# The SSM gate with its weights stationary, and bias rows written in eight transfers

## The reference, cut to what matters

```
y = gelu(y.reshape(bsz, L, SSM_WIDTH))                # SSM_WIDTH = 1024
y_ssm = y * sigmoid(y @ w_glu)                        # the gate, w_glu is 1024 x 1024
logits = q k^T * HEAD_DIM ** -0.5 + rel_bias[bucket]  # 16 heads, window 128
mixed = concat([rmsnorm(y_attn, attn_out_g), rmsnorm(y_ssm, ssm_out_g)])
x = x + mixed @ w_out
```

## Time and profile before

| | |
|---|---|
| median of 3 runs | 3362.72 us (3361.55 to 3363.08) |
| the profiled execution | 3362.97 us, of which its span 3360.9 us |
| mean granted TensorE clock | 0.984 |
| weights and all else read from HBM | 588.54 MB, 177 GB/s over the span |

### The profile page before, as it was taken

The page is one execution under the profiler, slowest core; times in us unless marked ns, Lnnn a source line. Parts: engine busy times, 40 slices in busy tenths (PEclk is TensorE's granted clock), DMA queues, the critical chain, the costliest instruction groups (busy, mean ns, idle before and its releaser), DMA issues. The chain is left out here.

```text
span 3360.9 us, 38629 instructions
## 1 busy us (share of the span) xinstructions
PE 3249.7 (97%) x15842; PEld 2672.1 (80%) x15842; DVE 1866.8 (56%) x1982; ACT 1473.6 (44%) x1759; POOL 80.3 (2%) x75
## 2 busy tenths in 40 slices
PE   7897999999999999999999999999999999999998
PEld 5775788888888778878888888878787788888886
DVE  6555555555545544665555555565555655555555
ACT  5534454444444444444444444444444544444443
POOL 1020000000000000000000000000000000000000
PEclk9998899999999999999999999999999999999999
DMA  7433355555555555555555555555454555555554
GB/s 192 139 108 119 125 188 188 189 190 195 191 188 192 183 170 188 194 165 198 191 191 188 188 188 188 189 165 186 140 175 161 175 186 190 189 188 188 188 188 150
DMA packets 187548, 596.28 MB, mean 177 GB/s; under 512 B 12491, under 2 KB 19308, under 8 KB 186860
## 3 DMA queue, kind: packets, MB, share of 16 engines
q1 hardware_dynamic: 187372, 593.82, 54.3%
HBM read 588.54 MB, written 5.23 MB: 177 GB/s over the span
## 5 line engine op out<-in xcount | busy, mean ns | idle before, releaser
L1086 DVE TENSOR_TENSOR LO<-RAW,HI 128x1024 fp32r<-128x1024 f32 (+1 forms) x1104 | 1346.6, 1222 | 1146.4 <-ACT HI L580 1144.2
L580 ACT ACTIVATE HI<-RAW 128x1024 fp32r<-128x1024 f32 (+1 forms) x1104 | 1159.0, 1052 | 1371.0 <-PE PS L1905 1354.1
L1905 PE MATMUL PS<-HI,KPA 128*128 128x512 f32 x5376 | 1497.4, 395 | 15.1 <-DVE JK L1732 4.3
L1905 PEld LDWEIGHTS PS<-HI,KPA 128*128 128x128 f32 x5376 | 1008.4, 190 | 229.2 <-issue 13.0
L1905 PE MATMUL PS<-HI,KPB 128*128 128x512 f32 x3392 | 935.9, 392 | 3.5 <-DVE ACC L1619 3.4
L1905 PE MATMUL PS<-LO,KPA 128*128 128x512 f32 x2688 | 840.5, 393 | 7.6 <-DVE LO L1086 6.3
L1905 PEld LDWEIGHTS PS<-HI,KPB 128*128 128x128 f32 x3392 | 631.6, 188 | 132.8 <-issue 5.0
L1905 PEld LDWEIGHTS PS<-LO,KPA 128*128 128x128 f32 x2688 | 508.5, 190 | 120.6 <-DVE LO L1086 9.0
L1905 PE MATMUL PS<-LO,KPB 128*128 128x512 f32 x1696 | 525.0, 391 | 0.0
L1905 PEld LDWEIGHTS PS<-LO,KPB 128*128 128x128 f32 x1696 | 318.7, 188 | 68.2 <-issue 0.5
L607 ACT ACTIVATE KPB<-PS 128x512 fp32r<-128x512 f32 x98 | 58.5, 598 | 181.3 <-PE PS L1930 181.3
(11 more groups left out here) (255 smaller groups left out, 962.3 us busy)
## 6 DMA issues: line engine op xcount, KB each, us to landing
RAW<-in_w_up SPq DMA_DIRECT2D x128, 1024.0 KB, 5.1
RAW<-in_w_down SPq DMA_DIRECT2D x128, 1024.0 KB, 5.5
RAW<-in_w_qkv SPq DMA_DIRECT2D x48, 1024.0 KB, 5.1
RAW<-in_w_ff_gate SPq DMA_DIRECT2D x88, 512.0 KB, 3.7
RAW<-in_w_ff_up SPq DMA_DIRECT2D x88, 512.0 KB, 4.6
RAW<-in_w_ff_down SPq DMA_DIRECT2D x44, 1024.0 KB, 5.5
RAW<-in_w_in_ab SPq DMA_DIRECT2D x40, 1024.0 KB, 4.9
RAW<-in_w_in SPq DMA_DIRECT2D x16, 1024.0 KB, 5.2
```

Of the source, the lines that this page charges most:

```text
L580: e.activation(HI[:, s % NSPLIT, 0:w], RAW[:, d % NRAW, j, 0:w], ACT.Copy).then_inc(S("hi_made"), 1)
L1086: e.tensor_tensor(LO[:, h, 0:w], RAW[:, d % NRAW, j, 0:w], HI[:, h, 0:w].bitcast(F32), ALU.subtract).then_inc(S("lo_made"), 1)
L1905: ins = e.matmul(PS[:, b + j, 0:cw], l, r[:, h, 512 * j:512 * j + cw], start=(i == 0 and part == 0), stop=(last and part == 2))
```

## The change

It has two parts. **Bias rows:** the one DMA at L511 becomes eight, of two rows each, put behind the weight pairs of u steps 6, 8, 10, 12, 14 and q steps 0, 2, 4. RB, OH and WV get memory of their own, since WV is read for longer; ScalarE's wait at L689 goes, and SyncE's waits ask for 128 in place of 16. **Gate:** in unit glu the weights (HI, LO) are the stationary side and the y chunk of 256 tokens moves; a step is 24 products of 256 columns, each with another stationary 128x128, into banks 0 to 3, with channels on partitions. It waits for HI, LO and both halves of the chunk before its first product. The sigmoid is taken in four pieces, the first three as their bank is done, and multiplied with yT; ScalarE and VectorE make the sT pairs straight from that, without transposes. Squares are taken per pair, and 16 products with a column of ones sum them over channels.

```diff
-        add("sT", 4, ("a", 4), "q", gain="ssm_g")
+        add("sT", 4, ("a", 4), "q", turned=False, gain="ssm_g")
...
+    RB, OH, WV = (sb(n, [128, w]) for n, w in (("RB", 16), ("OH", 383), ("WV", 383)))
+    ONE = sb("ONE", [128, 1])
...
-            if d == dma_of("u", 8):
+            if dma_of("u", 6) <= d < dma_of("u", 6) + 8:
+                h = 2 * (d - dma_of("u", 6))
                 q.wait_ge(S("bias_rows_made"), 1)
-                e.dma_start(scratch[:, :, 0:383], bcast(WV[0:16, :], 1, 128)).then_inc(S("bias_written"), 16)
+                e.dma_start(scratch[h:h + 2, :, 0:383], bcast(WV[h:h + 2, :], 1, 128)).then_inc(S("bias_written"), 16)
...
-                q.wait_ge(S("bias_written"), 16)
+                q.wait_ge(S("bias_written"), 128)
...
-            q.wait_ge(S("bias_written"), 16)
             spread_c(2, 2)
...
-        def ev_glu(t, b):
-            e.activation(ys[:, t, :], flat2(b), ACT.Sigmoid).then_inc(S("evac_act"), 1)
+        def gate_open(n):
+            u = U["glu"]
+            if n == 1:
+                q.wait_ge(S("tile0_done"), u.number + 1)
+            elif n == 3:
+                q.wait_ge(S("step_done"), u.last + 1)
+            else:
+                q.wait_ge(S("gate_banks"), n // 2 + 1)
+            done = S("evac_act") if n % 2 else S("gate_opened")
+            e.activation(GT[:, 2 * n:2 * n + 2, :].rearrange("p a b -> p (a b)"), PS[:, n, :], ACT.Sigmoid).then_inc(done, 1)
+
+        def s_feed():
+            g = G["sT"]
+            for j in range(4):
+                kt, ks = chunk(g, 2 * j)
+                q.wait_ge(S("gated"), j + 1)
+                q.wait_ge(S("step_done"), U[g.after].last + 1)
+                for c in range(2):
+                    ins = e.activation(kt[:, ks + c, 0, :], GT[:, 2 * j + c, :], ACT.Copy, scale=par(g.gain, 2 * j + c, 1))
+                ins.then_inc(S("chunk_hi"), 1)
+                yield
+
+        def s_squares():
+            yield
+            for n in range(4):
+                q.wait_ge(S("gated"), n + 1)
+                e.activation(SQS[:, 2 * n:2 * n + 2, :], GT[:, 2 * n:2 * n + 2, :], ACT.Square).then_inc(S("s_squared"), 1)
+                yield
...
+        qn = q_norm()
+        unit("glu", y_feed(), [S0, S1, qn], [qn], ahead=1)
+        sf = s_feed()
+        for n in range(3):
+            gate_open(n)
+        next(sf)
+        gate_open(3)
...
+        sS = s_squares()
+        unit("ws0", sf, [sS, att, att], [sS], have=1)
...
+        def gate_times(n):
+            u = U["glu"]
+            if n % 2:
+                q.wait_ge(S("evac_act"), u.ea[n // 2])
+            else:
+                q.wait_ge(S("gate_opened"), n // 2 + 1)
+            d = GT[:, 2 * n:2 * n + 2, :]
+            e.tensor_tensor(d, d, yT[:, 2 * n:2 * n + 2, :], ALU.mult).then_inc(S("gated"), 1)
...
+        att, sf = attn1(), s_feed()
+        for n in range(2):
+            gate_times(n)
+        q.wait_ge(S("gated"), 1)
+        next(sf)
+        for n in range(2, 4):
+            gate_times(n)
...
+            if u.name == "glu":
+                gate(u, i, h, kt, ks)
+                return
...
+        def gate(u, i, h, kt, ks):
+
+            last = i == u.nk - 1
+            q.wait_ge(S("chunk_hi"), G[u.group].first + i // 2 + 1)
+            q.wait_ge(S("lo_made"), u.first + i + 1)
+            q.wait_ge(S("chunk_lo"), G[u.group].first + i // 2 + 1)
+            for f in range(8):
+                if i == 0 and f % 4 == 0:
+                    was, wt = u.freed[f // 4]
+                    q.wait_ge(S("evac_act"), was.ea[wt])
+                w = slice(128 * f, 128 * f + 128)
+                for part, (l, r) in enumerate(((HI, 0), (HI, 1), (LO, 0))):
+                    ins = e.matmul(PS[:, f // 2, 256 * (f % 2):256 * (f % 2) + 256], l[:, h, w], kt[:, ks, r, :],
+                                   start=(i == 0 and part == 0 and f % 2 == 0), stop=(last and part == 2 and f % 2 == 1))
...
+        def s_sums():
+
+            for n in range(4):
+                yield
+            q.wait_ge(S("s_squared"), 4)
+            q.wait_ge(S("qk_turned_out"), 5)
+            q.wait_ge(S("pool_prep"), PP["one"])
+            for t in range(2):
+                for c in range(8):
+                    ins = e.matmul(PS[:, 6, t:t + 1], SQS[:, c, 128 * t:128 * t + 128], ONE[:, :], start=(c == 0), stop=(c == 7))
+            ins.then_inc(S("s_summed"), 1)
...
-        def back():
-            for n in range(4):
-                yield
-                for p in range(2):
-                    q.wait_ge(S(f"ssm{p}_out"), 4)
-                if n >= 2:
-                    q.wait_ge(S("y_back"), n - 1)
-                t, hf = n // 2, n % 2
-                for i in range(4):
-                    ins = e.transpose(PS[:, 6 + n % 2, i * 128:(i + 1) * 128], yT[:, 4 * hf + i, t * 128:(t + 1) * 128], ID[:, :])
-                ins.then_inc(S("y_turned"), 1)
...
-        unit("ws0", feed("sT", lambda c, t: ys[:, t, c * 128:(c + 1) * 128], s_ready), [att, att])
+        unit("ws0", None, [s_sums(), att, att])
```

## The result

| | before | after |
|---|---|---|
| median of 4 runs each, taken side by side | 3362.2 us | 3406.35 us (3405.32 to 3407.81) |
| span of the profiled execution | 3360.9 us | 3403.4 us |
| mean granted TensorE clock | 0.984 | 0.977 |

The ratio is 1.0131, 95% interval 1.0114 to 1.0149: the change costs 44 us. The forecast was 3415 with a range of 3398 to 3545.

A forecast was written before the change was run, and what follows sets the result against it. TensorE was busy for 97% of the span, with a stall where weights stood behind the bias write. Pieces +49, cold clock +2 and gate +1 made +52 us on 3362.97, so 3415, range 3398 to 3545.

The forecast's parts named there:

- slow at its source: Bias write from SBUF: its 99 GB/s, against 377 for loads, comes from its few source partitions, not lack of engines.
- The rate: Bias piece from two partitions: 99 GB/s divided by four, 24.8 GB/s, so 15.8 us a piece.
- The cycle: DMA queue in u and q: piece 15.8 plus weight pair 2.8, 18.6 us, eight times.
- The end of the stretch: Step q 6: last pair lands at 199 us, HI copy takes 1, start near 200 instead of 150.81: +49 us.
- The cold clock, +2: TensorE at step q 6: arrives from long pauses at 1.2 GHz, one step costs 2.0 us more.
- 1.5 - 2.1 + 0.9: Gate up to ws0: longer steps and LO waits +1.5 kept, first eight s transposes saved -2.1, VectorE's operations +0.9.
- the column sums: Gate's 16 one-column products, 32 weight loads: nothing to 32 x 0.1, half in TensorE's attention waits, +1.6 us.
- the -0.8 for the second eight s transposes: Gate: the other eight s transposes go, at eight in 0.8 us warm, saving 0.8 us.
- Two engines a piece: Rival for the bias pieces: two DMA engines carry each, 31.4 us a piece, 3540 us in all; chance 0.22.
- Pieces at the old rate: Rival for the bias pieces: 4.0 us each on all engines, the stall goes, 3346 us; chance 0.16.
- The high end of the gate: Rival in glu: weight loads bound each step, 14 us more, 3428; inside the likeliest case's 0.54.
- The signs named ahead: Bias landings 16 us or more, about 80 GB/s in 60 to 190 us, HI waiting nearly every pair, clock 0.5.

The follow-up runs named there:

- spread rows: New gate, one bias transfer, its 16 rows on partitions 0, 8, ..., 120: 3349.08 us; or the changed kernel, a piece's two rows eight partitions apart: 3360.59 us.
- one write: The changed kernel with its new gate, but the bias rows in one transfer behind the weight pair of u 8 as before: 3365.24 us, ratio 1.0011.
- the sums are away: New gate, pieces of 16 rows by 16 copies, with only two of the 16 column-sum products left: 3344.41 us, ratio 0.9947.
- all 128 partitions: New gate, one bias transfer, each row on eight neighbouring partitions and each partition sending 16 of the copies: 3349.17 us, ratio 0.9968.
- one partition for all engines: The changed kernel with each piece sent as two transfers of one row, one partition each: 3398.61 us, ratio 1.0103.

## Why the prediction was right or wrong

**The place and the mechanism: right.** The pieces of the bias rows are slow at their source, each weight pair waits behind one, and from u 10 on the DMA sets the pace. The runs with spread rows, which change only where the rows lie, show it; in the forecast "slow at its source" was an argument.

**The rate: right, in part by luck.** 24.8 GB/s was taken from a factor of 3.8 for eight times fewer partitions. The steady rate is 25 to 27 GB/s. The number of partitions is not what counts: 16 neighbours are four sources of 25 and two neighbours one, so that 99/4 was the right division; with the two rows of a piece eight apart the same reasoning would have been wrong by two (51 GB/s). The Trainium skill's account, which the forecast set beside its sum, was the better ground.

**The cycle: mis-sized, 18.6 us forecast, 15.9 measured.** Two things were missing in "15.8 + 2.8". A piece begins faster than it goes on: 47 to 51 GB/s for some 3.3 us (from 81 to 84 us), then 25, so it takes about 13. And only two engines have the piece; the other fourteen carry their share of the next pair meanwhile (253 GB/s in 84 to 88 us, beside a piece that began at about 81), so that what follows a piece is only the share of two engines, about 2.6 us (94 to 96 us: 51 GB/s in 25 packets at 13% of the engines). This is the term of the sum that was most off: eight cycles are 127 us and not 149.

**The end of the stretch: a term left out.** Eight cycles from 50 us gave 199 for the last pair; ScalarE's copy of it started at 177.06, which is 50 and eight cycles of 15.9. But the forecast then allowed 1 us to step q 6, and it was 9.8: that copy also lets VectorE go on with the SSM, whose 64 products at 1.2 GHz (6.32 us) TensorE does first. The two errors, 22 us early and 9 late, leave 13: +36.1 against +49. The cold clock, +2, measured 2.1 for the SSM products and 2.4 for the step.

**The gate: +1 forecast, +3.8 measured.** Up to ws0 the terms gave 1.5 - 2.1 + 0.9 = +0.3, measured +0.1, and term by term it holds in that trace: with one write q's turns start 1.1 us later than before (255.22 against 254.12), k's 2.15 (263.00 against 260.85), and the s transposes behind them are gone. The product spacing was 0.12 us as assumed, the LO waits 1.8 to 2.4 us three times instead of 1.1, and they are in part covered at q's turns, as the text had it. The failed term is the column sums: 32 x 0.11 = 3.55 us against the "nothing to 3.2", and the half taken as hidden in the waits of attention is not hidden at all, since the scores behind them find VectorE's logits no sooner or later than before; they also bring the clock down. 1.6 should have been some 3.5, and the -0.8 for the second eight s transposes shows as -0.1 at most (103.62 against 103.75 from ws0 to wa0 once the sums are away). Against it stands that ws0's first step now runs at the lower clock: 4.8 us with one write (268.38 to 273.17), 3.5 before (268.32 to 271.80).

**The rivals.** Two engines a piece: the engines were told rightly (share 0.12), the time for a packet wasn't. 0.23 us a packet before was an engine waiting for its part of four sources of 25 GB/s; with two engines on one it is 0.115. Pieces at the old rate: false for these pieces, but its consequence was right. With pieces that keep 16 rows the stall goes, and the kernel takes 3348 where the rival said 3346. The high end of the gate did not come.

**The signs named ahead.** HI waited for loads of w_in in every pair from u 10 to q 6, and the clock fell to 0.5 after the pauses (80 to 88, 181 to 186 us), as said. The DMA view gives no landing for the pieces; the third, issued at 68.18 us, has its last packets near 94. The traffic in 60 to 190 us was 104 GB/s and not about 80: a piece and a pair in 15.9 us are 91, and the rest was not traced.

**The sum.** 49 + 2 + 1 = 52 against 42.5 in the spans: some 12 too much in the cycle and its end (51 against the 39 that the pieces cost alone), some 3 too little in the gate. The forecast of 3415 is so nearer to the 3406 measured than its terms were: the errors have opposite signs.

## What to carry to other kernels

What a transfer out of SBUF reached here went by where its partitions lie (25 GB/s for two neighbours, 51 for two rows eight apart, 99 for 16 neighbours, 205 for 16 rows eight apart), and its slowest dimension decided how many engines had it. So cut a transfer along the dimension that leaves both as they were (copies and not rows here: the same eight pieces took the time from 3406 to 3348 us), or lay its rows out eight partitions apart. A slow transfer costs all that is queued behind it and the issuing engine too, so compare its cycle (transfer and what follows) with the interval at which the engines ask for loads in that very stretch (7.7 us here, and not the 12.3 of a later one). Products of one column are not small: 32 of them took 0.11 us each here. See whether anything waits behind them, and look at the clock after them.

## What the runs showed of the hardware that was not expected

- A transfer held back at its source begins faster than it goes on, at about what its engines carry. With two engines a piece has 66 packets in the first 2 us seen (97 to 99 us, 51 GB/s) and 17 a microsecond later (25 to 27 GB/s); with 16 engines the spread rows run at 391 GB/s in 56 to 58 us and at 205 from 60 us on. Two rows eight partitions apart, and all 128 partitions, show no such beginning: 51 and 400 GB/s throughout. What takes up the first part was not settled.
- With one partition for all engines, the 16 are 60 to 90% busy for 20 to 41 GB/s in all: their busy share contains waiting, and a share of 0.91 before was no sign that the engines were the limit.
- SyncE's issue of a 1 MB load, 0.37 us otherwise, lasts 13.4 us behind a piece; that the queue of the two engines is full then is a guess that no run shows.
- TensorE's granted clock fell to 0.50 after 32 one-column products that kept it busy by the trace, and stayed at 1.00 when four were left.
